# A hybrid gated-DeltaNet and attention layer: the recurrence split into a preparing phase and a scan, with 32x32 blocks inverted on GpSimd

## What is computed

```python
L = strict(beta * (k @ k.T) * decay)            # 128x128, strictly triangular
z = inv(I + L) @ (beta * (v - decay_row * (k @ S)))
o = decay_row * (q @ S) + (masked(q @ k.T * decay)) @ z
S = g_last * S + (k * decay_to_end).T @ z
```

## Time and profile before

| | us |
|---|---|
| median of 3 runs | 2053.45 (2053.3 to 2053.74) |
| span of the profiled execution | 2050.0 |
| PE / DVE / ACT / POOL busy | 1942.2 / 939.4 / 620.4 / 231.1 |

### The profile page before, as it was taken

The page is one execution under the profiler, slowest core; times in us unless marked ns, Lnnn a source line. Parts: engine busy times, 40 slices in busy tenths (PEclk is TensorE's granted clock), DMA queues, the critical chain, the costliest instruction groups (busy, mean ns, idle before and its releaser), DMA issues.

```text
span 2050.0 us, 39188 instructions
## 1 busy us (share of the span) xinstructions
PE 1942.2 (95%) x17278; PEld 1521.1 (74%) x17278; DVE 939.4 (46%) x1823; ACT 620.4 (30%) x1057; POOL 231.1 (11%) x385
## 2 busy tenths in 40 slices
PE   5679999999999999999999999899999889999999
PEld 2138888888777777777887877778887566678887
DVE  1323343565334555445445445575435644354333
ACT  4313222223143333222332322442235333322121
POOL 0000000000022222211112211311100101110000
PEclk9999999999999999999999999999999999999999
DMA  8872121223232222222221222667633222464333
GB/s 310 297 236 62 52 62 54 60 82 87 62 93 59 60 73 67 60 64 64 73 64 53 64 64 74 201 217 228 204 113 114 82 87 85 161 213 133 118 118 103
DMA packets 159474, 229.28 MB, mean 112 GB/s; under 512 B 10352, under 2 KB 108905, under 8 KB 157897
## 3 DMA queue, kind: packets, MB, share of 16 engines
q1 hardware_dynamic: 136841, 157.14, 25.9%
q0 software_dynamic: 14688, 55.48, 8.1%
q10 hardware_dynamic: 7776, 14.16, 1.9%
HBM read 203.15 MB, written 23.59 MB: 111 GB/s over the span
## 4 chain that ended last, share of the span: by engine, by line
PE 83%; DMA 6%; ACT 5%; DVE 4%; issue 2%; POOL 1%; SPq 0%; ACTq 0%; DVEq 0%; POOLq 0%
PE psum L1390 22%; PE psum L1392 20%; PE psum L1391 20%; DMA w_raw_mod<-w_mod_dram 3%; PE psum L1668 2%; PE psum L1457 2%; PE psum L1453 2%; PE psum L1514 1%; ACT inv L671 1%; PE psum L1465 1%; DVE w_lo L898 1%; PE psum L1420 1%; PE psum L1688 1%; PE psum L1655 1%; ACT w_hi L605 1%
## 5 line engine op out<-in xcount | busy, mean ns | idle before, releaser
L898 DVE TENSOR_TENSOR w_lo<-w_raw,w_hi 128x1024 fp32r<-128x1024 f32 x232 | 290.6, 1253 | 579.5 <-ACT w_hi L605 579.1
L605 ACT ACTIVATE w_hi<-w_raw 128x1024 fp32r<-128x1024 f32 x232 | 245.4, 1058 | 991.4 <-PE psum L1392 949.6
L1390 PE MATMUL psum<-h_hi,w_hi 128*128 128x512 f32 x1152 | 482.1, 419 | 13.8 <-DVE w_lo L898 11.6
L1392 PE MATMUL psum<-h_hi,w_lo 128*128 128x512 f32 x1152 | 454.1, 394 | 0.0
L1391 PE MATMUL psum<-h_lo,w_hi 128*128 128x512 f32 x1152 | 453.1, 393 | 0.0
L1390 PEld LDWEIGHTS psum<-h_hi,w_hi 128*128 128x128 f32 x1152 | 217.7, 189 | 56.2 <-DVE w_lo L898 8.3
L1392 PEld LDWEIGHTS psum<-h_hi,w_lo 128*128 128x128 f32 x1152 | 217.2, 189 | 50.5
L1391 PEld LDWEIGHTS psum<-h_lo,w_hi 128*128 128x128 f32 x1152 | 218.5, 190 | 33.0
L968 DVE SCALAR_TENSOR_TENSOR conv_acc<-conv_in,convw,conv_acc 128x772 f32<-128x772 f32 x96 | 98.2, 1023 | 3.4
L1390 PE MATMUL psum<-w_hi,m_hi 128*128 128x512 f32 x256 | 99.6, 389 | 0.0
L1391 PE MATMUL psum<-w_lo,m_hi 128*128 128x512 f32 x256 | 99.6, 389 | 0.0
(11 more groups left out here) (307 smaller groups left out, 2907.5 us busy)
## 6 DMA issues: line engine op xcount, KB each, us to landing
w_raw<-w_in_dram SPq DMA_DIRECT2D x168, 512.0 KB, 3.8
w_raw_mod<-w_mod_dram SPq DMA_DIRECT2D x64, 512.0 KB, 5.6
w_raw_modg<-w_mod_dram POOLq DMA_DIRECT2D x32, 512.0 KB, 4.4
w_raw<-w_out_dram SPq DMA_DIRECT2D x32, 512.0 KB, 3.7
gate_scratch<-gate_stage ACTq DMA_DIRECT2D x48, 256.0 KB, 3.9
w_raw<-w_proj_a_dram SPq DMA_DIRECT2D x16, 512.0 KB, 3.9
w_raw<-w_proj_b_dram SPq DMA_DIRECT2D x16, 512.0 KB, 3.7
gates<-gate_scratch POOLq DMA_DIRECT2D x32, 256.0 KB, 4.0
```

The source lines that it names most:

```text
L605: act.activation(part(whi[i % 2], p), part(place, p), ACT.Copy).then_inc(S("w_hi"), 1)
L898: dve.tensor_tensor(part(wlo[i % 2], p), part(raw_of(n)[0], p), part(whi[i % 2], p).bitcast(f32), ALU.subtract).then_inc(S("w_lo"), 1)
L1390: pe.matmul(out_ap, lh, rh, start=first, stop=False, skip_group_check=shared)
L1392: return pe.matmul(out_ap, ll, rh, start=False, stop=last, skip_group_check=shared)
```

## The change

Phase one prepares 12 **units** (a tile and four heads) in the order context tiles, then latent tiles 0, 3, 1, 2. A unit makes `gram`, `qk` and the transposed k once for both directions (four matmuls each in place of eight for a pair), both decays, L, and the transposed scores; SP stores L, scores and scaled k rows in DRAM (512 KB each), together with the 32x32 diagonal blocks of L (128 KB), which DVE cuts out and negates. A context unit takes 4 steps, a latent one 7. POOL loads the blocks of four units, one 32x32 block to a partition, inverts them by 30 steps of substitution (two instructions a step, the largest on 16x15 elements) and stores them. The first such batch is spread over the latent units, the other two follow. Six steps are left empty. Phase two is the scan: a pair keeps `couple5`, `correct5` (size 32), `couple6`, `correct6` (size 64), `ks`, `qs`, `z`, `az`, `kz`, in 11 steps (context) or 12 (latent), of which two to four have no slot. SP loads L, blocks, scores and k rows for the next pair; DVE transposes the blocks; ACT, no longer POOL, copies them into place. The first visit of an output tile writes it, so that the accumulator isn't cleared. The plan has 218 steps in place of 256; the 96 gate pieces stay. `load_L`, `load_k_rows` and `load_scores` are like `load_unit`, with 256 KB for each direction. The diff, cut to its core, without blank lines and set to the left:

```diff
-    pairs, slots = [], []
+    at, end = {}, 0
+    def slot(at_kk, **what):
+        at.setdefault(at_kk, []).append(what)
+    items = []
+    for tile in (LT, LT + 1, 0, 3, 1, 2):
+        for half in range(2):
+            lat, i = tile < LT, len(items)
+            it = dict(tile=tile, half=half, lat=lat, i=i, li=sum(o["lat"] for o in items), at=end)
+            items.append(it)
+            for m, k in enumerate(("kt", "decay", "gram", "qk", None, "at") if lat else ("kt", "decay", "gram")):
+                if k:
+                    slot(end + m, kind=k, item=i)
+            end += 7 if lat else 4
+    end += 6
+    pairs, n_slots = [], 0
     fwd = [LT, LT + 1] + list(range(LT))
     bwd = [LT + 1, LT] + list(range(LT))[::-1]
     for step in range(NT):
         for half in range(2):
             lat, last = step >= CT, step == NT - 1
-            pairs.append(dict(tiles=(fwd[step], bwd[step]), half=half, lat=lat, last=last, first=len(slots)))
-            p = len(pairs) - 1
-            early = p > 0
-            kinds = [("decay", 0)] + [("ks", 0)] * early + [("gram", 0)] + [("qk", 0)] * lat
-            for n in range(len(BLOCKS)):
-                kinds += [("couple", n)] + [("correct", n)] * (n > 0)
-            kinds += [("kt", 0)] * (not last) + [("ks", 0)] * (not early) + [("z", 0)]
-            kinds += [("at", 0), ("qs", 0), ("az", 0)] * lat + [("kz", 0)] * (not last)
-            slots += [dict(kind=k, n=n, pair=p, i=len(slots) + m) for m, (k, n) in enumerate(kinds)]
-            pairs[-1]["end"] = len(slots)
+            kinds = ["couple5", "ks", "correct5"] + (["qs"] if lat else [None])
+            kinds += ["couple6", None, "correct6", None, "z", None]
+            kinds += ["az"] * lat + ([None] if last else ["kz"])
+            pr = dict(tiles=(fwd[step], bwd[step]), half=half, lat=lat, last=last, at=end, first=n_slots)
+            for d in (0, 1):
+            pr["items"] = [[o["i"] for o in items if o["tile"] == pr["tiles"][d] and o["half"] == half][0] for d in (0, 1)]
+            for m, k in enumerate(kinds):
+                if k:
+                    slot(end + m, kind=k, pair=len(pairs), i=n_slots)
+                    pr[k] = n_slots
+                    pr["at_" + k] = end + m
...
+def load_unit(p):
+    pr = PAIRS[p]
+    for d in (0, 1):
+        sp.wait_ge(S("block_out"), 16 * (pr["items"][d] // 4 + 1))
+        if p:
+            sp.wait_ge(S(f"gp{d}"), PAIRS[p - 1]["correct5"] + 1)
+            sp.wait_ge(S("diag"), 2 * p)
+        dst = (XC, YC)[d][d]
+        sp.dma_start(dst[:], block_out[pr["items"][d], 4 * d:4 * d + 4].rearrange("u p j -> p u j")).then_inc(
+            S("inv_in"), 16)
...
+def scan_transfers(kk):
+    for u in UNITS:
+        i = u["i"]
+        if kk == u["at"] + 2:
+            sp.wait_ge(S("k_rows"), i + 1)
+            sp.dma_start(kr_scr[i], KR[:].rearrange("p d u n -> p d (u n)")).then_inc(S("k_rows_out"), 16)
+        if kk == u["at"] + 4:
+            for d in (0, 1):
+                sp.wait_ge(S("L"), 2 * i + d + 1)
+            sp.dma_start(l_scr[i], LL[:].rearrange("p d u n -> p d (u n)")).then_inc(S("l_out"), 16)
+            sp.wait_ge(S("diagonal"), i + 1)
+            sp.dma_start(block_in[i].rearrange("e p j -> p e j"),
+                         DIAG[:].rearrange("p d u j -> p (d u) j")).then_inc(S("block_in"), 16)
+        if u["lat"] and kk == u["at"] + 7:
+            for d in (0, 1):
+                sp.wait_ge(S("scoresT"), 2 * u["li"] + d + 1)
+            sp.dma_start(at_scr[u["li"]], AT[:].rearrange("p d u n -> p d (u n)")).then_inc(
+                S("scores_out"), 16)
+    if kk == PAIRS[0]["at"] - 6:
+        sp.wait_ge(S("block_in"), 16 * N_UNITS)
+        sp.wait_ge(S("diagonal"), N_UNITS)
+        load_unit(0)
+        sp.wait_ge(S("l_out"), 16 * N_UNITS)
+        load_L(0)
+        sp.wait_ge(S("k_rows_out"), 16 * N_UNITS)
+        load_k_rows(0)
+        sp.wait_ge(S("scores_out"), 16 * N_LAT)
+    for p, pr in enumerate(PAIRS[:-1]):
+        after = PAIRS[p + 1]
+        if kk == pr["at_correct5"] + 1:
+            load_unit(p + 1)
+        if kk == pr["at_couple6"] + 1:
+            load_L(p + 1)
+        if after["lat"] and kk == pr["at_z"] + 2:
+            load_scores(p + 1)
+        if not after["last"] and kk == pr["at_z"] + 3:
+            load_k_rows(p + 1)
...
+for q in range(4):
+    scan_transfers(4 * (n - 3 - N_GATE0 - 1) + q)
...
+def mask_scores(u):
     for d in (0, 1):
-        pool.wait_ge(S(f"gd{d}"), pr["first"] + 1)
         m = (GE, LE)[d]
+        pool.wait_ge(S("decayed"), 2 * u["li"] + d + 1)
         pool.tensor_tensor(DD[d][:], DD[d][:], consts[:, m:m + P].unsqueeze(1).to_broadcast([P, 4, P]),
-                           ALU.mult).then_inc(S(f"dmask{d}"), 1)
-    for d in (0, 1):
...
-        for q in range(4):
-            pool.tensor_copy(YY[d][32 * q:32 * q + 32, :, 32 * q:32 * q + 32], YC[d][32 * q:32 * q + 32]).then_inc(
-                S(f"diag{d}"), 1)
-        for q in (2 * d, 2 * d + 1):
-            c = 32 * (q % 2)
-            pool.tensor_copy(X64[32 * q:32 * q + 32, :, c:c + 32], XC[d][32 * q:32 * q + 32]).then_inc(
-                S(f"diag{d}"), 1)
-    for d in (0, 1):
-        pool.wait_ge(S(f"diag{d}"), 6 * (pi + 1))
+                           ALU.mult).then_inc(S("masked"), 1)
+steps = [0]
+def blocks_load(b):
+    pool.wait_ge(S("block_in"), 16 * 4 * (b + 1))
+    if b:
+        pool.wait_ge(S("block_out"), 16 * b)
+    pool.dma_start(BL[:].rearrange("p r j -> p (r j)"),
+                   block_in[4 * b:4 * b + 4].rearrange("i e (q r) j -> (i e q) (r j)", q=4)).then_inc(
+        S("blocks"), 16)
+    pool.wait_ge(S("blocks"), 16 * (b + 1))
+def block_steps(k0, k1):
+    for k in range(k0, k1):
+        outer = OUTER[:, 0:(31 - k) * k].rearrange("p (r j) -> p r j", j=k)
+        below = BL[:, k + 1:32, 0:k]
+        pool.tensor_tensor(outer, BL[:, k + 1:32, k:k + 1].to_broadcast([P, 31 - k, k]),
+                           BL[:, k:k + 1, 0:k].to_broadcast([P, 31 - k, k]), ALU.mult).then_inc(S("block_steps"), 1)
+        steps[0] += 2
+        pool.wait_ge(S("block_steps"), steps[0] - 1)
+        pool.tensor_tensor(below, below, outer, ALU.add).then_inc(S("block_steps"), 1)
+        pool.wait_ge(S("block_steps"), steps[0])
+def blocks_store(b):
+    pool.memset(BL[:].rearrange("p r j -> p (r j)")[:, 0:1024:33], 1.0).then_inc(S("block_steps"), 1)
+    steps[0] += 1
+    pool.wait_ge(S("block_steps"), steps[0])
+    pool.dma_start(block_out[4 * b:4 * b + 4].rearrange("i e (q r) j -> (i e q) (r j)", q=4),
+                   BL[:].rearrange("p r j -> p (r j)")).then_inc(S("block_out"), 16)
+decay_rhs(UNITS[0])
+pool.memset(X64[:], 0.0).then_inc(S("inv_zero"), 1)
+pool.wait_ge(S("kv_spill"), 16 * NT)
+pool.memset(SS[:], 0.0).then_inc(S("states0"), 1)
+for u in UNITS:
+    if u["i"] + 1 < N_UNITS:
+        decay_rhs(UNITS[u["i"] + 1])
+    if u["lat"]:
+        mask_scores(u)
+        if u["li"] == 0:
+            blocks_load(0)
+        block_steps(1 + 4 * u["li"], min(31, 5 + 4 * u["li"]))
+blocks_store(0)
 for d in (0, 1):
-    pool.wait_ge(S(f"gd{d}"), len(SLOTS))
+    pool.wait_ge(S("decay_mm"), 2 * N_UNITS)
+    pool.memset(YY[d][:], 0.0).then_inc(S("inv_zero"), 1)
+for b in (1, 2):
+    blocks_load(b)
+    block_steps(1, 31)
+    blocks_store(b)
...
+def prepare(slot):
+    k, u = slot["kind"], UNITS[slot["item"]]
+    i = u["i"]
+    if k == "kt":
+        act.wait_ge(S("k_rows_mm"), i + 1)
+        if i:
+            act.wait_ge(S("k_rows_out"), 16 * i)
+        for d in (0, 1):
+            for w in range(4):
+                h = 4 * u["half"] + w
+                ins = act.activation(KR[:, d, w, :], bank4(7)[:, w, :], ACT.Copy,
+                                     scale=DEC[:, u["tile"] * 2 + d, 1, h:h + 1])
+        ins.then_inc(S("k_rows"), 1)
+    elif k == "decay":
+        for d in (0, 1):
+            act.wait_ge(S("decay_mm"), 2 * i + d + 1)
+            if i:
+                act.wait_ge(S("L"), 2 * i)
+            if u["li"]:
+                act.wait_ge(S("scoresT_mm"), 2 * u["li"])
+            act.activation(DD[d][:], bank4(4 + 2 * d), ACT.Exp).then_inc(S("decay"), 1)
...
+def diagonal_blocks(p):
+    for d in (0, 1):
+        act.wait_ge(S("inv32"), 2 * p + d + 1)
+        if p:
+            act.wait_ge(S(f"gp{d}"), PAIRS[p - 1]["z"] + 1)
+        else:
+            act.wait_ge(S("inv_zero"), 3)
+        for q in range(4):
+            act.activation(YY[d][32 * q:32 * q + 32, :, 32 * q:32 * q + 32], YC[d][32 * q:32 * q + 32],
+                           ACT.Copy)
+        for q in (2 * d, 2 * d + 1):
+            c = 32 * (q % 2)
+            ins = act.activation(X64[32 * q:32 * q + 32, :, c:c + 32], XC[d][32 * q:32 * q + 32], ACT.Copy)
+        ins.then_inc(S("diag"), 1)
...
+def prepare(slot):
+    k, u = slot["kind"], UNITS[slot["item"]]
+    i, tile, half = u["i"], u["tile"], u["half"]
+    if k == "gram":
+        dve.wait_ge(S("gram_mm"), i + 1)
```

(117 more changed lines are left out.)

308 lines of the change are left out of this document (142 added, 166 removed).

## The result

The changed kernel takes **1983.44 us** (median of 4 runs, 1979.17 to 1991.43) against 2053.59 for the kernel before in the same session, a ratio of 0.966 (0.963 to 0.969): 70 us less, where 88 were forecast. It lies inside the range and inside the likeliest case's own, 1945 to 1990.

A forecast was written before the change was run, and what follows sets the result against it. PE was taken to bound the kernel: 119 us of PE work and 27 us of old waits go, 58 us of new waits come, so 2053.45 - 88.3 = 1965 us; likeliest case 1945 to 1990, 8-in-10 range 1925 to 2022.

The forecast's parts named there:

- the 108 small slots: Recurrence: nine small slots of each of 12 pairs go, at 0.90 us each, 97.2 us of PE work.
- the halved ones: `gram` and `qk` become 20 slots with four matmuls where 20 had eight: 0.91 us each, 18.2 us go.
- the rival in which the steps are not paced by PE: Small slots filled time DVE needs, so only the halved slots count: about 2040 us, or no gain; chance 0.03.
- the one in which POOL becomes the bound: POOL's substitution steps run slowly on short rows, 2 us an instruction: +139 us, 2104 us; chance 0.07.
- latent `at`: PE waits before the transposed scores of eight latent units, behind DVE's cuts and POOL's masks: 3.5 us each, 28 us.
- clock: Lower granted PE clock after waits in the latent units: 2 us for each of eight, 16 us, bounds 0 and 28.
- junction, context units: Waits for stores and loads between the two phases and in context units: 4 us, bounds 0 and 15.
- scan: Phase two: PE waits, with `ks`, `qs` and `kz` having one gate block against DVE's work: 10 us, bounds 0 to 30.
- The sentence on the weights: SP blocks on L before issuing the next weights, wanted about two pieces later, so a 4 us lag costs nothing.
- the weights-late rival: Weights come late behind waits and stores in SP's queue, 9.2 us in each latent unit: 74 us, 2039 us; chance 0.07.
- The lock of DVE and POOL: Latent units: each of eight cuts waits for a POOL step instruction of 0.55 us: 35 us, 2000 us; chance 0.18.
- a sign of being wrong: The prediction counted itself wrong if the part after the recurrence changed by over 5 us.

The follow-up runs named there:

- x6_before_short: The kernel before, with eight of nine small slots of each pair (block sizes 2 to 16) left out: 1958.56 us against 2055.24.
- x1_order: The changed kernel with DVE doing the score multiplies ahead of the diagonal cuts in latent units: 1944.25 us, ratio 0.945.
- y1_diag: The changed kernel with multiplies before cuts, second buffers for L, k rows and cut blocks, latent units of nine steps, context units of five: 1918.30 us.

## Why the prediction was right, and where it was off

**The two large terms held.** These are the 108 small slots at 0.90 (96 of them gave 96.7 us in `x6_before_short`, where 86.4 was the pure price) and the halved ones (17.3 us of PE work for 18.2). The scan ran within 2 us of the sum of its slots and gate blocks, and PE was its bound throughout, so the rival in which the steps are not paced by PE is out. So is the one in which POOL becomes the bound: means of 0.24 to 0.92 us by shape, batch 3 at 929.9, 242 us spare.

**The new waits were mis-sized: 58 forecast, 79 measured.** Term by term:

| term | forecast | measured | what the runs showed |
|---|---|---|---|
| latent `at` (3.5 x 8) | 28 | 37.7 | the mechanism, order in DVE, is right (`x1_order`: 24 us of it go); the first unit waits 9.5, behind 5.7 of DVE for L's single buffer; the other seven 4.0 each |
| clock | 16 | 27 | 0.53 us for each us of wait, not 2 a unit |
| junction, context units | 4 | 12.5 | 2.6 at the junction; 8.1 for w_lo and 1.8 for `gram`, in the context units and the first latent one |
| scan | 10 | 1.9 | PE waits for nothing in it; 0.7 of the 1.9 is its first gate block, at a lower clock behind the wait at the junction |

What was wrong in the **transfers** is a term that the sum lacks: the single buffers of L and of the k rows. The prediction sets only the cut blocks against their store ("the next cut is a unit away, at least 7.9 us"); that DVE and ACT must wait for the stores of L and k rows before they may write the next unit has no working of its own, and only the 4 us for junction and context units stand near it. The sentence on the weights, that a lag of 4 us costs nothing, held: no engine waits for a raw weight piece in phase one. It took 3.8 us for 512 KB from the loads of the weight stream; these stores landed later, L's at 5.1 us after its issue. Issues after, columns as in the earlier trace rows:

```profile
k_rows_scratch<-k_rows SPq DMA_DIRECT2D x12, 512.0 KB, 5.4
L_scratch<-L SPq DMA_DIRECT2D x12, 512.0 KB, 5.1
...
block_in_scratch<-L_diagonal SPq DMA_DIRECT2D x12, 128.0 KB, 5.3
```

In a context unit of four steps the store of L isn't in when DVE wants the buffer again. The timeline of such a unit in the changed kernel:

```profile
636.52 2.16 DVE L1143 SCALAR_TENSOR_TENSOR L<-psum,crow,decay 128x128 f32<-128x128 f32 x8 [5.83 <-DMA L_scratch<-L]
638.79 3.58 DVE L1155 TENSOR_TENSOR L_upper<-L,consts 32x128 f32<-32x128 f32 x4
639.04 1.09 POOL L552 TENSOR_TENSOR decay_rhs_lo<-consts,g_lo 128x512 fp32r<-128x512 f32 x1
640.09 1.08 POOL L552 TENSOR_TENSOR decay_rhs_hi<-consts,g_hi 128x512 fp32r<-128x512 f32 x1
641.14 1.08 POOL L552 TENSOR_TENSOR decay_rhs_lo<-consts,g_lo 128x512 fp32r<-128x512 f32 x1
642.41 1.17 DVE L1155 TENSOR_TENSOR L_diagonal<-L,consts 32x128 f32<-32x128 f32 x4
...
643.83 1.18 DVE L1048 TENSOR_TENSOR w_lo<-w_raw,w_hi 128x1024 fp32r<-128x1024 f32 x1
645.15 0.54 PE L1560 MATMUL psum<-h_hi,w_hi 128*128 128x512 f32 x1 [3.56 <-DVE w_lo L1048]
```

5.8 us of waiting for the store, then four cuts of 3.58 us in place of 1.17, beside three right-hand sides of POOL, then the `lo_part`, for which PE has stood 3.56 us. The raw weights were there: the `lo_part` starts as soon as DVE is free. It is the weights-late rival's effect (PE waits for w_lo) with another cause, DVE's order, and 8 us in place of 74.

**The lock of DVE and POOL** was a rival at 35 us. It is there, but between other instructions than the rival named. Its partners were to be POOL's steps, and with those left out of the changed kernel nothing changes; they meet the cuts only once the cuts are moved (`x1_order` and after). In the changed kernel it is the right-hand sides that meet the cuts, in the rows above for 2.4 us, and the `lo_part` that meets the masks, 2.2 us for 1.26. The cuts' groups in the changed kernel and, after them, in `x1_order`:

```profile
L1155 DVE TENSOR_TENSOR L_upper<-L,consts 32x128 f32<-32x128 f32 x48 | 20.3, 423 | 2.0 <-DVE L L1143 0.5
L1155 DVE TENSOR_TENSOR L_diagonal<-L,consts 32x128 f32<-32x128 f32 x48 | 13.6, 283 | 0.9
```

```profile
L1141 DVE TENSOR_TENSOR L_upper<-L,consts 32x128 f32<-32x128 f32 x48 | 36.4, 759 | 0.8
L1141 DVE TENSOR_TENSOR L_diagonal<-L,consts 32x128 f32<-32x128 f32 x48 | 21.5, 449 | 0.9
```

283 ns is the free price, as estimated (0.29). In `x1_order` the cuts fall beside masks and steps and take 24 us more of DVE in all, and the kernel is 32 us faster: what waits for them there is one `lo_part`, and PE 2.0 us for it. That DVE and POOL shut each other out for a whole instruction, as the Trainium skill has it (SBUF — State Buffer, "SBUF: two separate sides"), agrees with the four cuts stretched to 3.58 us beside three instructions of 1.08; that it must cost time doesn't follow, only that it does where the loser is waited for.

**Outside the recurrence** two things were taken as fixed, and they nearly cancel. One of them is a sign of being wrong that the prediction itself named: that the part after the recurrence changes by over 5 us. From the start of the first step, 607.0 before and 618.0 after, the profiled execution lost 11.0 us in front of the change. The program there is the same, and other runs start phase one at 606.3, so this is scatter of that execution, about the difference between its 1987.11 and the 1976.65 of the repeat. And the rest after the recurrence gained 8.6 us, after allowing for the 39 steps left for it at 1.351: the w_lo waits behind the recurrence are 5.3 us, 2.8 at most, for 9.6 and 5.7, and the clock that those had cost goes with them. Why they shrink wasn't tried. The sum: recurrence 672.9 - 552.7 - 52.7 = -67.5, start +11.0, rest -8.6, together -65.1. So the recurrence alone gained 67.5 us where 88.3 were forecast, 21 less, all of it in the new waits. Of these 21 the gain of the rest, which nothing in the prediction foresaw, made good 8.6; to that extent the nearness of the median to 1965 is luck.

**What stays open**: whether the w_lo waits of `y1_diag` go when POOL's steps are kept away from the cuts, why the rest gained 8.6 us, and the start's scatter of 13 us, larger than several effects measured here.
